# Everything behind the constants moved 16 columns on in SBUF

## The reference

```python
h = rms_norm(x, norm_g)
proj = h @ w_in
...
branch_d = jnp.einsum('nbsw,nwd->bsnd', ys, w_branch)
g = jax.nn.sigmoid(gates.reshape(bsz, s, N_BRANCH, d))
merged = jnp.sum(g * branch_d, axis=2)
return x + merged @ w_out
```

```python
merged = jax.nn.sigmoid(gate_f) * y_f + jax.nn.sigmoid(gate_d) * y_d
return merged @ w_out
...
return (jax.nn.silu(x_blk @ w_gate[e]) * (x_blk @ w_up[e])) @ w_down[e]
```

## Time and profile before

| | |
|---|---|
| runs | 1172.75, 1171.09, 1166.39 us |
| median | 1171.09 us |
| profiled execution, span | 1167.6 us (its own time is not given beside the span) |
| TensorE busy | 1019.9 us, 87% |
| VectorE busy | 506.4 us, 43% |
| POOL busy | 427.5 us, 37% |
| ScalarE busy | 380.4 us, 33% |
| read from HBM | 302.67 MB, 260 GB/s over the span |

### The profile page before, as it was taken

The page is one execution under the profiler, slowest core; times in us unless marked ns, Lnnn a source line. Parts: engine busy times, 40 slices in busy tenths (PEclk is TensorE's granted clock), DMA queues, the critical chain, the costliest instruction groups (busy, mean ns, idle before and its releaser), DMA issues.

```text
span 1167.6 us, 20205 instructions
## 1 busy us (share of the span) xinstructions
PE 1019.9 (87%) x8173; PEld 802.9 (69%) x8173; DVE 506.4 (43%) x980; ACT 380.4 (33%) x572; POOL 427.5 (37%) x192
## 2 busy tenths in 40 slices
PE   8999999999999999999999899966767667666685
PEld 6999999999999999797989797423323232332231
DVE  4346965601136887767854543222222222222213
ACT  5554354444447656334343344100000000000002
POOL 6767868888876866143031281000000000000000
PEclk9999999999999999999999899988888888888898
DMA  7644546566656544215220889999999999999995
GB/s 248 219 129 146 178 129 187 175 192 186 183 178 196 165 146 137 59 37 217 93 80 12 326 293 383 388 425 428 429 427 428 429 427 429 428 428 429 428 420 202
DMA packets 43569, 304.75 MB, mean 261 GB/s; under 512 B 5092, under 2 KB 5476, under 8 KB 30952
## 3 DMA queue, kind: packets, MB, share of 16 engines
q1 hardware_dynamic: 43208, 303.21, 69.1%
q10 hardware_dynamic: 288, 0.52, 0.1%
HBM read 302.67 MB, written 1.05 MB: 260 GB/s over the span
## 4 chain that ended last, share of the span: by engine, by line
PE 57%; DMA 27%; DVE 8%; POOL 2%; issue 2%; ACT 2%; SPq 2%; DVEq 0%; ACTq 0%; POOLq 0%
DMA arena<-gate_up 24%; PE bank L484 11%; PE bank L485 11%; PE bank L486 10%; PE bank L1357 6%; PE bank L862 5%; PE bank L1378 3%; POOL rounded L2966 1%; DMA weights<-front 1%; DMA arena<-down 1%; PE bank L826 1%; DVE arena L2091 1%; POOL rounded L2925 1%; SPq L3010 1%; PE bank L1097 1%
## 5 line engine op out<-in xcount | busy, mean ns | idle before, releaser
L2925 POOL TENSOR_TENSOR rounded<-weights,rounded 128x1024 fp32r<-128x1024 f32 x152 | 370.4, 2463 | 156.3 <-ACT rounded L1443 146.9
L484 PE MATMUL bank<-rounded 128*128 128x256 f32 (+2 forms) x776 | 219.2, 282 | 2.2 <-POOL rounded L2925 2.2
L485 PE MATMUL bank<-rounded 128*128 128x256 f32 (+2 forms) x776 | 216.5, 279 | 0.0
L486 PE MATMUL bank<-rounded 128*128 128x256 f32 (+2 forms) x776 | 216.2, 279 | 0.0
L1443 ACT ACTIVATE rounded<-weights 128x1024 fp32r<-128x1024 f32 x146 | 147.4, 1052 | 80.6 <-PE bank L486 47.6
L484 PE MATMUL bank<-rounded,rounded 128*128 128x256 f32 (+3 forms) x552 | 158.3, 287 | 2.1 <-DVEq L2346 0.8
L485 PE MATMUL bank<-rounded,rounded 128*128 128x256 f32 (+3 forms) x552 | 156.2, 283 | 0.0
L486 PE MATMUL bank<-rounded,rounded 128*128 128x256 f32 (+3 forms) x552 | 156.1, 283 | 0.0
L484 PEld LDWEIGHTS bank<-rounded 128*128 128x128 f32 (+1 forms) x776 | 145.6, 188 | 4.3 <-POOL rounded L2925 2.9
L485 PEld LDWEIGHTS bank<-rounded 128*128 128x128 f32 (+1 forms) x776 | 145.5, 187 | 0.7 <-issue 0.6
L486 PEld LDWEIGHTS bank<-rounded 128*128 128x128 f32 (+1 forms) x776 | 145.2, 187 | 0.0
(11 more groups left out here) (465 smaller groups left out, 1456.6 us busy)
## 6 DMA issues: line engine op xcount, KB each, us to landing
weights<-front SPq DMA_DIRECT2D x165, 512.0 KB, 4.2
arena<-down SPq DMA_DIRECT2D x31, 2048.0 KB, 22.0
weights<-gate_up SPq DMA_DIRECT2D x28, 2048.0 KB, 34.7
arena<-gate_up SPq DMA_DIRECT2D x28, 2048.0 KB, 33.4
weights<-front SPq DMA_DIRECT2D x4, 2048.0 KB, 8.0
weights<-gate_up SPq DMA_DIRECT2D x8, 768.0 KB, 12.5
arena<-gate_up SPq DMA_DIRECT2D x4, 1536.0 KB, 33.7
weights<-gate_up SPq DMA_DIRECT2D x4, 512.0 KB, 7.3
```

Source lines behind the costliest of these rows:

```text
L484: nc.tensor.matmul(out, a[0], b[1], start=start, stop=False)
L485: nc.tensor.matmul(out, a[0], b[0], start=False, stop=False)
L486: return nc.tensor.matmul(out, a[1], b[0], start=False, stop=stop)
L2925: nc.gpsimd.tensor_tensor(lo, raw[q % RAW], hi.bitcast(f32), ALU.subtract).then_inc(sem("w_lo"), 1)
```

## The change

The place where all stages begin is rounded up to a multiple of 32 columns (128 bytes) instead of 8. The columns before it end at 3727; so `layer_base` becomes 3744 instead of 3728, and every tile placed from it lies 16 columns (64 bytes) further on. Ring, constants and the tiles at the arena's end stay.

```diff
@@ -125,7 +125,7 @@
         stats = place(256)
         rows = place(N_ROWS)
         tri = place(4 * P)
-        top[0] = layer_base = -(-top[0] // 8) * 8
+        top[0] = layer_base = -(-top[0] // 32) * 32
 
         def col(name, j=0):
             a = COLS[name][0]
```

## The result

The changed kernel takes 1175.34 us (median of 19 runs, 1169.56 to 1177.82) against 1170.75 us for the kernel before (19 runs, 1166.39 to 1175.45). The medians differ by 4.6 us. The ratio of the two kernels is 1.0035, with a 95% interval of 1.0024 to 1.0045: 4.1 us, between 2.8 and 5.3.

What follows compares the result with a forecast made beforehand. TensorE was taken to set the pace up to about 714 us, then the HBM stream. Terms 2.4 + 2.5 - 0.8 + 0.3 - 0.1 = +4.3 us on 1171.1 gave 1175.4 us, range 1166 to 1180.

Steps and rivals of the forecast that it cites:

- Distance of the operands, not their place: Rounded products on TensorE: their spacing depends on how both operands lie to each other, 113.3 to 120.0 ns.
- The 2016 products at 117.8: Stage one products of activations h1 spaced 117.8 ns slow to 119.0, 1.2 ns each: +2.4 us.
- in step: Both operands of a product equally far from 128-byte multiples; spacing taken as 119.0 ns, bounds 118.6 and 120.0.
- The 432 at 113.3: Products of h1 in dq, av, half of au, cx and cz lose 5.7 ns each: +2.5 us.
- Hidden behind VectorE: From about 98 to 165.8 us the chain avoids TensorE, so slower products there do not count: -0.8 us.
- Closing parts: Closing products before the expert loop: parts 8 to 15 lose 0.55 + 0.1 us, half counted: +0.3 us.
- wf: Stage two's 96 products on yf_hi and yf_lo, leaving equal operand offsets, gain 1.2 ns each: -0.1 us.
- Median for median: The profiled execution's own time was not given, so +4.3 us was added to the runs' median, 1171.1 us.
- All at 120.0: Rival: every h1 stream locks at 120.0 ns, +6.2 us, 1177.3 us; chance 0.25.
- nothing changes: Rival: h1's streams keep 113.3 and 117.8 ns as they fall, 1171 us; chance 0.15.
- whole units free every stream: Rival: with operands on 128-byte multiples all h1 streams run at 113.3 ns, -7.4 us, 1163.7 us; chance 0.16.
- the fast rival: Rival with all h1 streams at 113.3 ns: 7.0 us gained plus half of 0.8 in closing products; chance 0.16.

Runs made afterwards that it cites:

- the two runs with everything moved: Weights ring and arena both 16 columns further on, once on the kernel before (ratio 0.9997), once on the changed kernel (ratio 1.0027 to the kernel before).
- the kernel with three splits: Kernel before, with one product split into 48 and 208 columns heading two gate blocks and the first branch product: 1166.62 us, again 1166.95.

## Why the prediction was right

The forecast was 1175.4 us, the measurement 1175.34; and it came by the mechanism that was forecast, more than by its sizes. That the two agree to 0.1 us is luck: the interval of the ratio spans 2.8 to 5.3 us, the forecast of +4.3 was put on a median of three runs (1171.09; 19 runs give 1170.75), and the spacings of the one profile after account for 3.9.

- **Distance of the operands, not their place.** Shown by the two runs with everything moved. In kernels that differ only in where the stages begin, 1104 products take 129.54, 130.03, 131.01 or 132.48 us at 32, 64, 0 and 96 bytes. The Trainium skill's rule of independent read ports ("TensorE: Matmul & The Clock Gate", Part 2), by which loading the next weights takes no read bandwidth from the running matmul, would lead one to expect no difference; for the pace of these products the measurement decides against it.
- **The 2016 products at 117.8.** I took 119.0 for in step, 2.4 us. It was a mixture: the gates at 118.7, bz to cc at 120.0. Over the streams of stage one the sum is 2.1 us.
- **The 432 at 113.3.** All lost it: 2.4 us, forecast 2.5. This term rests on one profile's share of fast streams, and later profiles of the same operands have other shares (dq, dv, av, cx and cz fast or slow in turn). Another profile would have given another term: with none of them fast, the change would have cost about 1.7 us less (the 384 that are not hidden, at 4.45 ns).
- **Hidden behind VectorE.** Forecast 0.8; the spacings of that stretch sum to 0.8 and its length grows by 0.08. TensorE's wait for POOL's splits up to w_out falls as foreseen, but little, from 2.2 us in two waits (2.9 with the third, behind w_out) to 1.8:

```profile
PE bank L484 <- POOL rounded L2925: 1.8, 2, 1.1
```

- **Closing parts.** Forecast 0.3 of 0.65 left: 0.5 lost, 0.4 of it taken up behind, in one profile. Of the 96 products that the prediction puts at 113.3, shows 48; the other 48, parts 8 and 9, took 5.44 us as well (684.52 to 689.96 us of before).
- **wf.** Forecast -0.1 for all four at 117.8; two reached 113.6, about -0.2 more.
- **Median for median.** The forecast put the difference on the median though the profile's own time was unknown; this was needed, since the two profiles lie 3.9 us apart by half-clock episodes alone.
- **The rivals.** All at 120.0 came true in part (bz to cc, cz), and at 96 bytes for all of h1 but dv and av (118.8 and 117.5), where the ratio is 1.0042. That nothing changes, and that whole units free every stream, fell: 118.6 is the best that distance 0 showed. In the fast rival's sum the 0.8 us of the closing parts is too much: the 72 at 117.8 would gain 0.3, the 24 in step 0.2.

## What to carry to other kernels

Read the spacing of back-to-back products from long stretches before taking matmul time as fixed: here it depends on where moving and stationary operand lie to each other modulo 128 bytes, by up to 6% (113.3 to 120.0 ns). At 32 and at 64 bytes the kernel took the same time (ratio 0.9999), though only 64 showed 113.3; at 0 and at 96 it took 0.3 to 0.4% more. Aligning both operands to the same boundary is not a gain in itself; it was the loss here. A term that rests on which streams one profile found fast is a draw: several profiles are needed to size it. Where two profiles of a kernel are compared, first take out the stretches whose granted clock differs.

## What the runs showed of the hardware that I had not expected

- The distance is signed: 32 bytes gave 117.3 ns and 96 gave 120.0, and exchanging the operands' parts exchanges them.
- At 64 bytes two speeds, 113.3 and 117.8, exist for the same instructions, and which one a stream takes differs between executions. The stream keeps it for 1104 products, through transposes at the heads of its blocks; a product split at 48 columns can change it in either direction.
- Episodes of half clock come and go between executions of the same code: of the two profiles of the kernel with three splits, one has the clock at 0.83 between 80 and 90 us, the other at 1.00.
